# Attention scores of both query tiles made in one go, in a two-layer hybrid encoder on one core

## What is computed

```python
def one_block(args):
    q_blk, i = args
    ...
    logits = jnp.einsum("bqhmd,bkhmd->bhmqk", q_blk, k).astype(jnp.float32) * scale
    p = jax.nn.softmax(logits + bias[None, :, None], axis=-1)
    attn = p[:, :, 0] - lam * p[:, :, 1]
    return jnp.einsum("bhqk,bkhe->bqhe", attn.astype(v.dtype), v)
```

## Time and profile before

| | |
|---|---|
| time, median of 3 runs | 1746.02 us (1744.76 to 1748.0) |
| span of the profiled execution, first to last instruction | 1742.8 us |
| PE busy in the whole span | 1694.6 us, 97% |
| DVE, ACT, POOL busy | 713.3, 685.1 and 668.0 us |
| the stage of attention and scan, layer 0 | about 197 to 300 us of the span |
| the same stage, layer 1 | about 1062 to 1165 us |
| granted TensorE clock in both stages | full (1.00, 2.4 GHz) |

### The profile page before, as it was taken

How to read it: one execution, slowest core, us unless ns; L and a number is a source line. 1 busy time by engine, 2 the same in 40 slices (tenths; PEclk the granted TensorE clock), 3 DMA queues, 4 the chain that set the end, 5 groups by cost and what they waited for, 6 DMA issues and landing times.

```text
span 1742.8 us, 23270 instructions
## 1 busy us (share of the span) xinstructions
PE 1694.6 (97%) x8975; PEld 1056.7 (61%) x8975; DVE 713.3 (41%) x1345; ACT 685.1 (39%) x1549; POOL 668.0 (38%) x536
## 2 busy tenths in 40 slices
PE   8999999999999999899999999999999999999997
PEld 6889877787434444343378898777864344443343
DVE  5728788524212212121276387865241212222122
ACT  5565787754211111111156567877541111111111
POOL 7888876894000000000077887768930000000000
PEclk9999999999999999999999999999999999999999
DMA  7554312667999999999954442227589999999997
GB/s 271 195 193 152 140 49 108 274 259 308 363 415 427 428 427 428 427 428 428 411 229 165 179 189 97 97 80 300 219 333 398 420 427 427 428 427 428 428 425 303
DMA packets 50707, 528.47 MB, mean 303 GB/s; under 512 B 5496, under 2 KB 8312, under 8 KB 20128
## 3 DMA queue, kind: packets, MB, share of 16 engines
q1 hardware_dynamic: 50560, 526.89, 74.2%
q0 software_dynamic: 32, 0.02, 0.0%
HBM read 525.82 MB, written 1.06 MB: 302 GB/s over the span
## 4 chain that ended last, share of the span: by engine, by line
PE 68%; DMA 9%; DVE 9%; SPq 5%; ACT 5%; issue 2%; POOL 1%; DVEq 0%; ACTq 0%
PE PS L1297 19%; PE PS L1325 10%; DMA view<-in_w_exp_down_dram 9%; PE PS L875 8%; PE PS L877 8%; PE PS L876 8%; SPq L678 5%; DVE view L2003 5%; PE PS L1237 2%; PE PS L1223 1%; DVE view L1999 1%; PE PS L1082 1%; PE PS L1224 1%; PE PS L863 1%; ACT view L1571 1%
## 5 line engine op out<-in xcount | busy, mean ns | idle before, releaser
L2370 POOL TENSOR_TENSOR view<-view,view 128x512 fp32r<-128x512 f32 x448 | 579.8, 1315 | 548.1 <-ACT view L1457 537.3
L1297 PE MATMUL PS<-view,view 128*64 128x512 f32 x2044 | 457.8, 600 | 15.1 <-issue 14.5
L1457 ACT ACTIVATE view<-view 128x512 fp32r<-128x512 f32 x448 | 275.1, 633 | 149.1 <-PE PS L877 146.9
L1297 PEld LDWEIGHTS PS<-view,view 128*64 128x64 f32 x2044 | 150.9, 138 | 292.0 <-issue 288.7
L875 PE MATMUL PS<-view,view 128*128 128x512 f32 x704 | 286.0, 406 | 5.6 <-POOL view L2370 3.7
L877 PE MATMUL PS<-view,view 128*128 128x512 f32 x704 | 275.5, 391 | 0.0
L876 PE MATMUL PS<-view,view 128*128 128x512 f32 x704 | 275.4, 391 | 0.0
L1325 PE MATMUL PS<-view,stb 128*64 128x512 f32 x1024 | 230.4, 597 | 8.4 <-DMA view<-in_w_exp_down_dram 5.5
L2270 DVE SCALAR_TENSOR_TENSOR view<-PS,gcol,view 128x512 fp32r<-128x512 f32 x64 | 48.1, 751 | 448.7 <-ACT view L1770 448.6
L875 PEld LDWEIGHTS PS<-view,view 128*128 128x128 f32 x704 | 132.8, 189 | 33.5 <-issue 5.8
L1325 PEld LDWEIGHTS PS<-view,stb 128*64 128x64 f32 x1024 | 71.3, 136 | 132.6 <-issue 117.0
(11 more groups left out here) (260 smaller groups left out, 2024.0 us busy)
## 6 DMA issues: line engine op xcount, KB each, us to landing
view<-in_w_exp_up_dram SPq DMA_DIRECT2D x56, 2048.0 KB, 25.8
view<-in_w_exp_down_dram SPq DMA_DIRECT2D x56, 2048.0 KB, 28.1
view<-in_w_mix_dram SPq DMA_DIRECT2D x54, 2048.0 KB, 7.7
view<-in_w_exp_gate_dram SPq DMA_DIRECT2D x52, 2048.0 KB, 28.8
view<-in_w_exp_gate_dram SPq DMA_DIRECT2D x20, 512.0 KB, 31.2
view<-in_w_exp_down_dram SPq DMA_DIRECT2D x20, 512.0 KB, 14.9
view<-in_w_exp_gate_dram SPq DMA_DIRECT2D x8, 1024.0 KB, 8.1
view<-in_w_exp_up_dram SPq DMA_DIRECT2D x8, 1024.0 KB, 9.3
```

The lines of the kernel that those rows point to most:

```text
L1297: ins = pe.matmul(bank(ph, name, j)[e * CAP:(e + 1) * CAP, :], xgT1[:, k, at + e * CAP:at + (e + 1) * CAP], rows, start=(k == 0), stop=(k ...
L1457: nc.scalar.activation(highs(chunk), weights(slot8, chunk), ACT.Copy).then_inc(*high_ready.up(ph))
L2370: g_.tensor_tensor(weights(low8, chunk), weights(slot8, chunk), highs(chunk), ALU.subtract).then_inc(*low_ready.up(ph))
```

## The change

The scores of a head are made once, at its even step: four matmuls, both query tiles times both maps. Query tile 0 goes into the first 256 columns of banks 6 and 7, query tile 1 into the other 256. At the odd step PE makes no scores. DVE evicts its half in each step; only the eviction of the odd step frees the banks. Since the even eviction no longer counts as one of the bank, DVE's wait for its own result goes by `link` there, which is why `dve_step` counts eight more. SP's one wait for the last scores names the same eviction by its new number.

```diff
-            f += [(("D", j, q), 4), (("sc", i), 6)]
+            f.append((("D", j, q), 4))
+            if q == 0:
+                f.append((("sc", j), 6))
...
-        dve_step = sig("dve_step", 279, 0)
+        dve_step = sig("dve_step", 287, 0)
...
-                        sp.wait_ge(*out_of(ph, "sc", ATT - 1))
+                        sp.wait_ge(*out_of(ph, "sc", HEADS - 1))
...
-                def scores(i):
+                def scores(h):
 
-                    h, qt = i // 2, i % 2
-                    pe.wait_ge(*free(ph, "sc", i))
-                    if i == 0:
+                    pe.wait_ge(*free(ph, "sc", h))
+                    if h == 0:
                         pe.wait_ge(*out_of(ph, "xT", XT))
-                    for m in range(2):
-                        rows = slice(m * HD, (m + 1) * HD)
-                        ins = pe.matmul(PS[:, 6 + m, 0:TT * P], qT[rows, h, qt * P:(qt + 1) * P], kT[rows, h, :],
-                                        start=True, stop=True)
-                    ins.then_inc(*fill(ph, "sc", i))
+                    for qt in range(TT):
+                        for m in range(2):
+                            rows = slice(m * HD, (m + 1) * HD)
+                            ins = pe.matmul(PS[:, 6 + m, qt * TT * P:(qt + 1) * TT * P],
+                                            qT[rows, h, qt * P:(qt + 1) * P], kT[rows, h, :], start=True, stop=True)
+                    ins.then_inc(*fill(ph, "sc", h))
...
                             decay_sums(i)
-                            scores(i)
+                        if i and q == 0:
+                            scores(j)
...
-                        dve.wait_ge(*full(ph, "sc", i))
+                        dve.wait_ge(*full(ph, "sc", h))
...
-                        v.scalar_tensor_tensor(out=lg[:, i % 2], in0=PS[:, 6:8, 0:TT * P],
-                                               scalar=HD ** -0.5, in1=bias, op0=ALU.mult, op1=ALU.add
-                                               ).then_inc(*drain(ph, "sc", i))
-                        dve.wait_ge(*out_of(ph, "sc", i))
+                        ins = v.scalar_tensor_tensor(out=lg[:, i % 2], in0=PS[:, 6:8, qt * TT * P:(qt + 1) * TT * P],
+                                                     scalar=HD ** -0.5, in1=bias, op0=ALU.mult, op1=ALU.add)
+                        if qt:
+                            ins.then_inc(*drain(ph, "sc", h))
+                            dve.wait_ge(*out_of(ph, "sc", h))
+                        else:
+                            link(ins)
```

## The result

Over 21 runs each the changed kernel takes 1748.47 us and the kernel before 1745.55 us (medians). The ratio is 1.0019, with a 95% interval from 1.0012 to 1.0025; it leaves out one slow run of the kernel before, of 2440.25 us. That is a small loss, near the bound of what can be told: 2.1 to 4.4 us. Forecast was +2.9 us; the medians differ by 2.92. The profiled execution has a span of 1745.9 us, against 1742.8 before.

The account below looks back on a forecast made before the run. PE bounds the stage, with ACT and DVE close behind. 3 x 0.43 + 2 x 0.07 = +1.43 us a layer, +2.9 in two, carried over to the median of 1746.0: 1748.9 us, range 1744.0 to 1753.5.

Parts of the forecast that it names:

- the relays: Three chains from an odd step's decay sums: PE's own row, ACT to o (0.35 us spare), DVE to the transposes (0.21).
- The saving of an odd step: Scores dropped at odd steps: PE alone would save 0.63 us, but o waits for ACT's eviction, so 0.36 stays.
- the five steps named: Odd steps 3, 7, 9, 11 and 15, where o was to wait for ACT's eviction of the transposes.
- The gap ahead of the scores: Between the decay sums and the scores of an odd step: at most 0.15 us more falls away.
- The cost of an even step: Two added score matmuls run as pairs side by side and cost PE 0.43 us, four taking 1.06.
- the most open term: Rival: the four scores do not run side by side, an even step costs 0.85 us, total 1753.1; chance 0.2.
- Steps 3 to 5 and 11 to 13: DVE sets the transposes of steps 5 and 13, so PE's -0.36 and +0.43 us do not count there.
- step 2: Even step whose added scores push PE by 0.43 us, with nothing to absorb it.
- y at step 16: Matmuls that wait 0.68 us for DVE, which hangs on step 15's decay sums, so step 15's saving does not count.
- Passed on whole: Behind the stage, PE's whole shift of +2.9 us reaches the kernel's end, not swallowed by the DMA-bound expert stage.
- DVE's relief is worth nothing: DVE's line 2035 of an odd step can start up to 2.32 us earlier, but line 2050 still waits for ACT.

Follow-up runs that it names:

- The removal alone: Changed kernel with even steps making only query tile 0's scores, which DVE evicts in both steps: ratio 1.0014 to the kernel before; run again, 1.0019.
- the addition alone: Kernel before, with two more score matmuls (results unused) in each even step and the odd steps' scores kept: ratio 1.0023.
- the eviction by DVE: Changed kernel with DVE instead of ACT evicting the transposes at steps 3, 7, 9, 11 and 15: ratio 1.0016 to the kernel before.
- the order by maps: Changed kernel with the four scores ordered map 0 tile 0, map 0 tile 1, map 1 tile 0, map 1 tile 1: ratio 1.0019 to the kernel before.
- the padding: Kernel before, with twenty more score matmuls behind the y matmuls of step 16 in each layer: 1753.65 us against 1745.03, ratio 1.0046.
- the two moves: One product piece put ahead of the transposes at steps 5 and 13, in the kernel before (ratio 0.999) and in the changed kernel (ratio 0.9998).
- all together: Changed kernel with the product pieces moved, DVE evicting transposes at five odd steps, and head 1's scores at step 1: ratio 1.0009; run again, 0.9995.

## Why the prediction was right

- **What bounds the stage**: right. PE is nearly full, and the half that was removed was worth 1 us in the two stages, not 11, because ACT and DVE hold PE as soon as it gets ahead. The removal alone, the addition alone and the eviction by DVE gave -0.48, +2.1 and +1.03 us a layer where the relays said -0.3, +2.15 and +0.95.
- **The saving of an odd step**, 0.36 instead of 0.63 us: decay sums to decay sums it is 0.37 (step 3, from +0.39 to +0.02). The wait of o for ACT is there in the five steps named. One more hand-over was close: the bank of the decay sums, which was the next to bite in the eviction by DVE.
- **The gap ahead of the scores**, up to 0.15 us, fell away as bounded: decay sums to off takes 219.08 - 218.14 = 0.94 us instead of the 1.09 from one decay sums' start to the scores. The rule of the Trainium skill (TensorEngine Tiling (Array Packing), Key Properties), that a change of the tiling mode drains the array, agrees with it; no run separates a drain from another cause of the 0.15 us.
- **The cost of an even step**, 0.43 us: 1.06 for four, as said. That it did not come out at 0.85 was the most open term; the order by maps shows that it was not a matter of neighbours either.
- **Steps 3 to 5 and 11 to 13 swallow what lies in them**: right, +0.38 at step 5 and +0.99 at step 13.
- **A small miss**: step 2 was counted 0.43 and is 0.33. In the kernel before, y to the transposes took 1.81 us there and 1.73 in step 4, so 0.09 us of slack may have absorbed it. It does not show at the end, since other terms are off by as little the other way.
- **Another**: the prediction names no new wait of the transposes at step 15, but they wait for DVE in the changed kernel (PE's shift is +0.89 there, where the saving alone, 1.44 - 0.78, would give +0.66). It costs nothing, because y at step 16 hangs on DVE.
- **Passed on whole**: right within the scatter, shown with the 4.5 us of the padding.
- **DVE's relief is worth nothing**: right; the waits for PE fell from 8.1 to 2.2 us, those for ACT grew by 8.6.

The expectations of the two moves were off by a third to a half where they used a gap between weight loads as idle time, and that of all together with them. The prediction used the same measure for step 5, but there only its sign mattered.

## What to carry to other kernels

Removing a wait helps only if the waiting engine is late for what comes next; read the row behind the wait before pricing the wait. Where three engines hand work round in a loop and each has a few tenths of a microsecond to spare, price a saving as the smallest slack on the way, but an added piece in full, so moving work from one step to the next can be a loss even if its sum gets smaller. The time set free is not gone: independent work moved into the new wait got more of it back than in the kernel before (1.76 against 0.71 us a layer). Judge a small change by the length of its own stage, which one trace gives to 0.1 us as long as the granted clock stays full in it, and use the run times only to see whether the rest stayed the same.

## What the runs showed of the hardware

- Four fp32 score matmuls of 64 rows and 256 columns take 1.06 us in either order of the row halves; two take 0.63. The fixed part of such a group is 0.2 us, and each pair more costs 0.43.
- A weight load that waits does not start under the running matmul as the others do, so the gap between two weight loads overstates idle time of the array: 0.69 us read, 0.38 us real.
- Every trace has stretches of 3.4 us at a granted clock of 1.2 GHz, one to five ahead of the last 10 us; where PE was busy throughout, one cost 1.4 us.
- The same program's DMA-bound expert stage varies by 1.7 and 2.7 us between two executions, while the stage before it repeats to 0.06 us.
- A program that differs only by fewer matmuls can show a gap of 1.8 to 2.4 us in PE, with no engine waited for, some 580 us behind the edited stage of layer 0 and 180 ahead of that of layer 1; after the longer one the granted clock fell to half for 3.4 us.
